# A two-layer diffusion step on one core: three units of the condition's map moved ahead of attention's first transpose, one to the third item, and a row copy ahead of the exponentials

## What is computed

```python
for l in range(DEPTH):                                     # DEPTH = 2
    sh1, sc1, gt1, sh2, sc2, gt2 = _modulation(silu_cond, w_ada[l], b_ada[l])   # the condition's map
    h = _rmsnorm(x, norm_mix_pre[l]) * (1.0 + sc1) + sh1
    y = mixer(h)                  # in-projection, four kinds of attention heads, out-projection
    x = x + gt1 * _rmsnorm(y, norm_mix_post[l])
    h = _rmsnorm(x, norm_ffn_pre[l]) * (1.0 + sc2) + sh2
    x = x + gt2 * _rmsnorm(_channel_mixer(h), norm_ffn_post[l])

def _modulation(silu_cond, w_ada_l, b_ada_l):
    m = (silu_cond @ w_ada_l + b_ada_l)[:, None, :]        # 1024 -> 6 * 1024
    return jnp.split(m, 6, axis=-1)
```

## Time and profile before

| | us |
|---|---|
| median of three executions | 1506.94 (1505.9 to 1507.28) |
| profiled execution, its device time | 1507.1 |
| profiled execution, its span | 1505.2 |
| PE busy in the span | 1470.7 (98%) |
| DVE busy | 1153.8 (77%) |
| ACT busy | 975.3 (65%) |

### The profile page before, as it was taken

The page is one execution under the profiler, slowest core; times in us unless marked ns, Lnnn a source line. Parts: engine busy times, 40 slices in busy tenths (PEclk is TensorE's granted clock), DMA queues, the critical chain, the costliest instruction groups (busy, mean ns, idle before and its releaser), DMA issues.

```text
span 1505.2 us, 20999 instructions
## 1 busy us (share of the span) xinstructions
PE 1470.7 (98%) x7205; PEld 1192.2 (79%) x7205; DVE 1153.8 (77%) x994; ACT 975.3 (65%) x963; POOL 122.2 (8%) x178
## 2 busy tenths in 40 slices
PE   8999999999998999999999999999999999999997
PEld 4867788886877788888888888888888888888885
DVE  2677554455568478888898888888888888888887
ACT  3555643435555457777777777777777777777774
POOL 2521410000030200000000000000000000000000
PEclk9999999999999989999999999999999999999998
DMA  9976976558760879999999999999999999999992
GB/s 362 354 247 209 346 251 198 189 171 287 256 239 4 322 283 377 409 384 385 379 377 378 389 379 379 384 376 376 392 372 375 394 377 364 401 373 367 394 395 104
DMA packets 222980, 489.10 MB, mean 325 GB/s; under 512 B 9392, under 2 KB 42496, under 8 KB 222928
## 3 DMA queue, kind: packets, MB, share of 16 engines
q1 hardware_dynamic: 215376, 466.38, 83.9%
q0 software_dynamic: 7552, 22.03, 4.6%
HBM read 479.53 MB, written 8.85 MB: 324 GB/s over the span
## 4 chain that ended last, share of the span: by engine, by line
PE 93%; DVE 3%; ACT 2%; issue 1%; DMA 0%; POOL 0%; DVEq 0%; ACTq 0%; POOLq 0%
PE ps L1899 24%; PE ps L1900 24%; PE ps L1904 24%; PE ps L1912 4%; PE ps L1913 3%; PE ps L1919 3%; PE ps L1950 2%; PE ps L2350 2%; PE ps L2129 1%; PE ps L2082 1%; PE ps L2104 1%; PE ps L2006 1%; PE ps L1961 1%; DVE sm L1436 0%; ACT region L927 0%
## 5 line engine op out<-in xcount | busy, mean ns | idle before, releaser
L1299 DVE TENSOR_TENSOR w_lo<-raw,w_hi 128x2048 fp32r<-128x2048 f32 (+1 forms) x397 | 905.7, 2285 | 172.1 <-ACT w_hi L874 170.9
L874 ACT ACTIVATE w_hi<-raw 128x2048 fp32r<-128x2048 f32 (+1 forms) x397 | 757.7, 1913 | 245.9 <-PE ps L1900 223.6
L1899 PE MATMUL ps<-w_hi,x_hi 128*128 128x512 f32 x1056 | 417.9, 396 | 1.4 <-DVE region L1526 1.4
L1900 PE MATMUL ps<-w_hi,x_lo 128*128 128x512 f32 x1056 | 411.7, 390 | 0.0
L1904 PE MATMUL ps<-w_lo,x_hi 128*128 128x512 f32 x1056 | 279.5, 389 | 0.0
L1899 PEld LDWEIGHTS ps<-w_hi,x_hi 128*128 128x128 f32 x1056 | 198.4, 188 | 42.4 <-DVE region L1526 1.8
L1904 PEld LDWEIGHTS ps<-w_lo,x_hi 128*128 128x128 f32 x1056 | 198.2, 188 | 41.7
L1900 PEld LDWEIGHTS ps<-w_hi,x_lo 128*128 128x128 f32 x1056 | 198.5, 188 | 39.5
L1899 PE MATMUL ps<-w_hi,h_hi 128*128 128x512 f32 x520 | 203.1, 391 | 0.0
L1900 PE MATMUL ps<-w_hi,h_lo 128*128 128x512 f32 x520 | 202.4, 389 | 0.0
L1904 PE MATMUL ps<-w_lo,h_hi 128*128 128x512 f32 x520 | 137.4, 389 | 0.0
(11 more groups left out here) (277 smaller groups left out, 1059.8 us busy)
## 6 DMA issues: line engine op xcount, KB each, us to landing
raw<-in_moe_w_gate SPq DMA_DIRECT2D x112, 1024.0 KB, 6.6
raw<-in_moe_w_up SPq DMA_DIRECT2D x112, 1024.0 KB, 6.7
raw<-in_moe_w_down SPq DMA_DIRECT2D x112, 1024.0 KB, 6.1
raw<-in_w_ada SPq DMA_DIRECT2D x48, 1024.0 KB, 8.6
raw<-in_w_in SPq DMA_DIRECT2D x20, 960.0 KB, 7.9
raw<-in_ffn_w_gate SPq DMA_DIRECT2D x22, 512.0 KB, 4.2
raw<-in_ffn_w_up SPq DMA_DIRECT2D x22, 512.0 KB, 5.7
raw<-in_ffn_w_down SPq DMA_DIRECT2D x11, 1024.0 KB, 5.0
```

What stands on the lines that cost most here:

```text
L874: act.activation(split_hi(c, slice(0, width(c))), raw[:, r % NRAW, 0:width(c)], ACT.Copy).then_inc(hi_done, 1)
L1299: dve.tensor_sub(split_lo(c, n), raw[:, raw_of(c) % NRAW, n], split_hi(c, n)).then_inc(lo_done, 1)
L1899: pe.matmul(out, xh, split_hi(c, w), start=start, stop=False, skip_group_check=True)
L1900: last = pe.matmul(out, xl, split_hi(c, w), start=False, stop=False, skip_group_check=True)
```

## The change

```diff
-ITEM_ADA = [{0: 12, 1: 13, 2: 14, 3: 15, 4: 16, 5: 17, 8: 18, 9: 19}, {8: 16, 9: 17}]
+FIRST_ADA = [(12, 13), (16,)]
+ITEM_ADA = [{2: 14, 3: 15, 4: 16, 5: 17, 8: 18, 9: 19}, {2: 17}]
...
                 for s, step in FIRST_BY[0]:
                     prep(l, s, step)
+                rows(l, 2 + l)
                 exps(l, 0)
                 act.wait_ge(lam_s, l + 1)
                 act.activation(lam[:, 2:4], lam[:, 0:2], ACT.Exp).then_inc(lam_e, 1)
-                rows(l, 2 + l)
                 exps(l, 1)
...
                 all_first_wait(pe, l)
+                for n in FIRST_ADA[l]:
+                    ada(l, n)
                 for i in range(10):
                     item_T(l, i)
```

## The result

The changed kernel takes 1509.83 us (median of nine executions, 1508.02 to 1512.67) against 1506.18 before: ratio 1.0024, 95% interval 1.0016 to 1.0032. On another chip, ten executions gave 1510.15 against 1506.13, ratio 1.0020 (1.0011 to 1.003). The kernel is slower by 3.6 to 4.0 us, 0.20 to 0.24%, and both intervals lie above 1. The forecast was 1507.4 with a range up to 1508.7. The 1506.18 is the median of nine executions of before; one of them took 2115.75 us and is left out of the ratio.

A forecast was written before the change was run, and what follows sets the result against it. PE was taken to bound the kernel, busy 98% of the span. Layer 0's +0.5 us, layer 1's 0 and zero for row copy and transfers, on a median of 1506.94, gave 1507.4 us, range 1505.7 to 1508.7.

The forecast's parts named there:

- what bounds the start of the items: Ahead of item 0, both layers: PE waits 1.60 us for DVE's C1 copy; units written behind it leave that wait empty.
- layer 0's lateness through DVE: Layer 0, item 3's transposes: DVE falls behind, `mod_ready` comes late, 0.49 us lost; taken as +0.5, bounds 0 and 1.0.
- the unit: Length of one moved unit on PE, taken as its pitch of 0.99 us; two ahead of item 0 cost 1.98 us.
- layer 1's order: Layer 1: unit 16 ahead of item 0 costs 0.99 us, unit 17 is free at item 2, item 9 returns 0.99; sum 0.
- the row copy: ACT's copy moved ahead of the exponentials: delays item 0's by at most 0.60 us, hidden; cost zero.
- no transfer was late: Layer 1's unit 16, asked for at 432.95, lands by 444.7 us, ahead of 445.43; transfers do not change the sum.
- the clock: Rival, 3%: PE's clock falls to half in the attention items, about 7 us lost, giving 1514 us.
- The sum: Whole kernel: +0.5 us on the median 1506.94, giving 1507.4 us.

The follow-up runs named there:

- ahead: The changed kernel with its first units written ahead of the wait for the preparations' copies instead of behind it; 1505.83 us against 1506.02 before, ratio 0.9999.
- l1_only: Kernel before with only layer 1's units 16 (ahead of item 0) and 17 (item 2) and the row copy moved; 1507.57 us, ratio 1.0008.
- l0_only: Kernel before with only layer 0's units 12 and 13 and the row copy moved, layer 1's table as before; 1507.92 us against 1505.94, ratio 1.0012.
- gap8: Kernel before with layer 1's unit 16 moved from item 8 to item 2, leaving item 8's wait open; median 1508.58 us, ratio 1.0011.
- fillers: Changed kernel plus unread matmuls: five at item 8 of layer 1, three ahead of item 3's transposes in layer 0; 1507.87 us against 1505.94, ratio 1.0009.
- gap8_fill: Kernel before with layer 1's unit 16 at item 2 and five unread matmuls at item 8 in its place; 1506.84 us against 1506.02, ratio 1.0002.
- copy_only: Kernel before with only ACT's row copy moved ahead of the exponentials in both layers, all units unmoved; 1506.31 us against 1506.13, ratio 1.0001.
- dense_l1: Kernel before with layer 1's units 16, 17, 18, 19 at items 2, 3, 4, 8, none ahead of the output projection; 1506.09 us against 1506.13, ratio 0.9996.
- spread: Kernel before with only layer 1's table changed: unit 16 at item 2, 17 at item 8, none in item 9; 1504.22 us against 1506.02, ratio 0.9990.
- best: Changed kernel, units 12 and 16 ahead of the wait, 13 at item 1, 17 and 18 at layer 1's items 2 and 8; 1506.52 us, ratio 0.9999.

## Why the prediction was wrong

**Right: what bounds the start of the items.** The 1.6 us wait for the C1 copy stayed whole in both layers, since the units stand behind it. ahead shows the counterpart: with the units in the wait, layer 0 takes 47.82.

**Right in kind, a little too large: layer 0's lateness through DVE.** Item 3's transposes wait for `mod`, 0.72 us. Counted from the C1 transposes they start 17.43 us in, 17.28 before: 0.15 late instead of 0.49. The term mis-sized is the unit: two in a row cost 1.86 (96.04 to 97.90), and each removed gave back 1.18 rather than 0.99 (item 0 went from 4.74 to 3.57 us, item 1 from 6.40 to 5.21). So item 1's transposes came 0.69 late and not 0.99. With the rest of the items the order costs 0.29, by the second profile.

**Right: layer 1's order.** Item 8's product is 1.00 us late (39.87 against 38.87 after C1), as the 0.99 said, and unit 17 was free at item 2. It is given back at item 9 where the clock is full: in l1_only, whose items 8 and 9 ran at full clock, the product starts 40.02 us after C1 and `out_T` 41.81, against 41.75 before.

```profile
481.98 1.08 PE L2130 MATMUL ps<-region 128*128 128x64 f32 x8 [1.51 <-DVE region L1466]
...
483.77 1.04 PE L2185 MATMUL ps<-cst,xn 128*128 128x128 f32 x8
```

The product with `w_o` is 0.30 late in that profile, but a fall over items 3 to 5 alone left 0.29 in l0_only, so what the order leaves at the end lies between 0 and 0.3. gap8, without the delay, has 46.58.

**Right: the row copy** costs nothing, and no transfer was late.

**Wrong: the clock.** It stood as a rival with 3%, the right mechanism, dismissed by "the rows, whose 1.60 us gaps left the clock at 1.00", and by the count that the new wait at item 8 was no longer than those. Two things failed in that step. It took one execution's 1.00 for a property of the order: the changed kernel's two profiles differ by 3.95 us in layer 1, with the same instructions. And it priced a fall by the only one it saw, 16 us and 7 us lost. The falls here are 3.4 us in layer 0 (0.9 us lost, 1.15 less 0.29), 3.4 in layer 1 (1.5) and 10.2 + 3.4 (5.5): 0.25 to 0.44 us lost for each, against the 0.44 taken, but on far shorter stretches. In the sum the clock stood at nothing. The Trainium skill ("TensorE: Matmul & The Clock Gate", section "Why this matters for your kernels") warns of idle gaps between bursts of matmuls, but of gaps longer than any in the items. By that rule as it stands item 8 is no danger, other than the prediction says. The runs show more than the rule: with a wait of 1.51 us open half of gap8's executions were slow, and with five matmuls in it none was.

**The sum** was +0.5 by order; measured by order it is 0.3, plus what of layer 1 is not given back. Of the 2.66 us in the first profile the clock has about 2.4, of the 5.75 in the second over 5. That the other 3 us of the median are the clock's too is inferred from these two and from fillers; the executions with 0.992 speak for a part that no profile shows. Open is also why the clock falls where it does. In l0_only, l1_only, gap8_fill and fillers it fell around items 3 to 5 of layer 1, in before, copy_only and gap8 (as profiled) not at all, with much the same instructions there.

## What to carry to other kernels

Small pieces of work that fill another engine's waits have a second use: they can keep the clock up at their place, though dense_l1 shows no guarantee. Before moving one out of a wait where it is hidden, because it "costs nothing there", look at how long PE then stands idle among small matmuls, and compare whole sets of executions, not two profiles. And a piece gains only in front of the wait it is to fill: one line lower it is added to it.

## What the runs showed of the hardware

- A fall of the clock on a stretch where DVE sets the pace is nearly free (0.29 us for 6.8 us at half clock in layer 1 of l0_only), while 3.4 us on a stretch that PE sets cost 0.9 to 1.5.
- The time at half clock ahead of the first expert product is 17.1 us in most profiles, but 6.8 in spread and 20.5 in best, and the way there takes 51.06, 49.78 and 52.66 us.
- The start of the program goes two ways, with the clock as well. Of 33 executions of before on the last chip 21 lie at 1505.6 to 1506.5 and 12 at 1507.1 to 1507.7. The profile of before, with 1507.1 us like the upper group, has the clock at half for 6.8 us from about 8 us on, that of the changed kernel for 3.4, and the C1 transposes stand at 95.23 and 93.84. In fillers (95.10) 3.4 us at half clock lie at 28 to 32 us instead, so the place counts too. First before, then the changed kernel:

```profile
12.00:14.00 2.00, 2.00 (x10) 0.20 (x8) 0.00 (x0) 2.00 (x4) 0.80 (x2) 0.50 1.04 403
```

```profile
12.00:14.00 2.00, 2.00 (x12) 0.87 (x12) 0.00 (x0) 2.00 (x4) 0.80 (x2) 0.89 1.05 405
```
